# Differential attention run two heads at a time between the products that make q, k and v, with part of the output projection in its drain

## The reference

```python
q, k, v = jnp.split(h @ w_qkv, 3, axis=-1)       # h: 256 latent and 256 context tokens of 1024
s1 = einsum("bqhd,bkhd->bhqk", q1, k1) * scale    # 8 heads, each with two halves of 64
s2 = einsum("bqhd,bkhd->bhqk", q2, k2) * scale
p = softmax(s1) - lam * softmax(s2)
o = einsum("bhqk,bkhe->bqhe", p, v)
y = (rms_norm(o, subln_g) * (1 - lam_init)).reshape(b, s, D_MODEL) @ w_o
```

## Time and profile before

| what | value |
|---|---|
| median of 3 runs | 3429.49 us (3424.19 to 3432.53) |
| the profiled execution, its time | 3427.78 us |
| its span | 3426.5 us |
| mean granted clock of TensorE, of full speed | 0.962 |
| PE busy | 3164.6 us (92%) |
| DVE busy | 1747.6 us (51%) |
| ACT busy | 1449.8 us (42%) |
| POOL busy | 997.9 us (29%) |

### The profile page before, as it was taken

The page is one execution under the profiler, slowest core; times in us unless marked ns, Lnnn a source line. Parts: engine busy times, 40 slices in busy tenths (PEclk is TensorE's granted clock), DMA queues, the critical chain, the costliest instruction groups (busy, mean ns, idle before and its releaser), DMA issues.

```text
span 3426.5 us, 50565 instructions
## 1 busy us (share of the span) xinstructions
PE 3164.6 (92%) x21050; PEld 2685.3 (78%) x21050; DVE 1747.6 (51%) x2989; ACT 1449.8 (42%) x2388; POOL 997.9 (29%) x440
## 2 busy tenths in 40 slices
PE   5999998995789999799988989999999989999899
PEld 3777776773567777558988987777989977879899
DVE  3353334236453332665656655665456455654565
ACT  3442223224342222554445444655444456554443
POOL 0212212201111113003433432343443422434433
PEclk9999999996799999899999999999999999999999
DMA  8344444421145554104544543332445532334454
GB/s 282 123 135 160 160 160 144 163 74 50 37 148 172 172 169 149 53 25 136 185 133 130 190 138 111 99 99 87 151 145 176 181 117 85 101 99 151 147 183 148
DMA packets 469299, 459.97 MB, mean 134 GB/s; under 512 B 9040, under 2 KB 467664, under 8 KB 469072
## 3 DMA queue, kind: packets, MB, share of 16 engines
q1 hardware_dynamic: 465760, 453.32, 41.7%
q10 hardware_dynamic: 3312, 3.42, 0.3%
HBM read 455.66 MB, written 1.05 MB: 133 GB/s over the span
## 4 chain that ended last, share of the span: by engine, by line
PE 78%; DVE 11%; ACT 6%; issue 3%; POOL 1%; DMA 0%; ACTq 0%; DVEq 0%; POOLq 0%; SPq 0%
PE bank L398 22%; PE bank L399 21%; PE bank L400 21%; PE bank L442 3%; ACT wh L345 2%; DVE wl L361 2%; DVE hl L706 1%; PE bank L1403 1%; DVE sm L1249 1%; PE bank L1394 1%; PE bank L2141 1%; PE bank L1015 1%; PE bank L456 1%; DVE bc L2181 1%; POOL sq L514 1%
## 5 line engine op out<-in xcount | busy, mean ns | idle before, releaser
L373 POOL TENSOR_TENSOR wl<-raw,wh 128x768 fp32r<-128x768 f32 (+1 forms) x336 | 880.1, 2620 | 2148.2 <-ACT wh L345 2138.3
L345 ACT ACTIVATE wh<-raw 128x2048 fp32r<-128x2048 f32 x336 | 636.2, 1894 | 326.8 <-PE bank L400 311.4
L361 DVE TENSOR_TENSOR wl<-raw,wh 128x1280 fp32r<-128x1280 f32 (+1 forms) x336 | 499.0, 1485 | 425.2 <-ACT wh L345 416.3
L398 PE MATMUL bank<-nh,wh 128*128 128x272 f32 (+1 forms) x1712 | 509.9, 298 | 23.6 <-DVE nl L1726 22.8
L398 PE MATMUL bank<-xh,wh 128*128 128x512 f32 (+2 forms) x1312 | 463.8, 353 | 44.5 <-ACT xh L562 32.9
L400 PE MATMUL bank<-nh,wl 128*128 128x272 f32 (+1 forms) x1712 | 497.3, 290 | 0.0
L399 PE MATMUL bank<-nl,wh 128*128 128x272 f32 (+1 forms) x1712 | 495.8, 290 | 0.0
L399 PE MATMUL bank<-xl,wh 128*128 128x512 f32 (+2 forms) x1312 | 456.0, 348 | 0.0
L400 PE MATMUL bank<-xh,wl 128*128 128x512 f32 (+2 forms) x1312 | 455.0, 347 | 0.0
L398 PEld LDWEIGHTS bank<-nh,wh 128*128 128x128 f32 x1712 | 330.4, 193 | 40.1 <-issue 37.8
L398 PE MATMUL bank<-hh,wh 128*128 128x512 f32 (+1 forms) x1024 | 350.3, 342 | 3.4 <-DVE X L614 1.9
(11 more groups left out here) (408 smaller groups left out, 5634.1 us busy)
## 6 DMA issues: line engine op xcount, KB each, us to landing
raw<-in_mlp_w SPq DMA_DIRECT2D x128, 1024.0 KB, 5.3
raw<-in_mod_w SPq DMA_DIRECT2D x83, 1024.0 KB, 5.2
raw<-in_w_in SPq DMA_DIRECT2D x60, 1024.0 KB, 5.3
raw<-in_w_mlp_up SPq DMA_DIRECT2D x32, 1024.0 KB, 5.7
raw<-in_w_mlp_down SPq DMA_DIRECT2D x32, 1024.0 KB, 5.3
raw<-in_w_in SPq DMA_DIRECT2D x34, 512.0 KB, 4.1
raw<-in_w_ssd_down SPq DMA_DIRECT2D x16, 1024.0 KB, 5.2
early<-in_mod_w SPq DMA_DIRECT2D x13, 1024.0 KB, 11.9
```

What stands on the lines that cost most here:

```text
L345: nc.scalar.activation(self.wtile(self.wh, c1), self.rawtile(c1), AF.Copy).then_inc(*up("act_wh", ("wh", c1)))
L361: nc.vector.tensor_tensor(l, r, h.bitcast(F32), ALU.subtract).then_inc(*up("dve_wl", ("wl_dve", c1)))
L373: nc.gpsimd.tensor_tensor(l, r, h.bitcast(F32), ALU.subtract).then_inc(*up("pool_wl", ("wl_pool", c1)))
L398: nc.tensor.matmul(o, ah, bh, start=first, stop=False)
```

## The change: what it does

Two heads' q, k and v are made by one chunk each, and the chunks now come in the order q0, k0, v0, q1, k1, v1 and so on. As soon as two heads are there, their units of attention run between quarters of the next chunks (a quarter is half a group of q or k, 12 matmuls, or one tile of v, 24 narrow ones): `beat` gives two steps for three quarters. Steps 0 to 26 stand there; steps 27 to 36 are the drain. In steps 29 to 32 of the drain stand the first six of eight tiles of four groups of `wo` (`pe_wo`); their last two tiles and the other four groups follow after step 36. One step holds, on PE: the turn of unit s-2, the scores of unit s, the product with v of unit s-3 and, every fourth time, the turn of a head's output.

Within a step the work is different too. The scores have one pair of banks of PSUM, not two. DVE no longer scales both exponentials: it joins them in one instruction and leaves the division by the first sum to ACT, which applies it in four copies of 128 columns per head. All copies to `dpt` are ACT's. The root is taken on DVE for each head, from an integer guess and three refinements, eleven small instructions before the scaling; ACT loads no tables for it. The low part of the output is one DVE instruction on the bank. Four modulation chunks that stood after chunks of `wo` stand in the drain (steps 27, 28, 34, 35).

```diff
+            for j in range(4):
+                for i, p in enumerate("qkv"):
+                    w(("qkv", p, j), a["diff_w_qkv"][0], 0, 8, 1024 * i + 256 * j, 256)
+                    mods(2, 3 * j + i, 3 * j + i + 1)
+            mods(2, 12, 16)
...
+    def beat(self, w, j, half):
+        n = 12 * j + 4 * "qkv".index(w) + half - 8
+        return 2 * (n // 3) + n % 3 // 2 if n >= 0 and n % 3 != 1 else None
...
+                    for half in range(4):
+                        m = half // 2
+                        if half % 2 == 0:
+                            o = self.pe_bank((0, 1), "dqk", w, 2 * j + m)
+                        cs = slice(128 * m, 128 * m + 128)
+                        for k in range(4 * (half % 2), 4 * (half % 2) + 4):
+                            ins = self.mm3(o[:], hi[:, k, cs], lo[:, k, cs], XH[:, k, :], XL[:, k, :], k == 0, k == 7)
+                        if half % 2:
+                            ins.then_inc(*up("pe_acc", ("acc", "dqk", w, 2 * j + m), *([("used", c)] if m else [])))
+                        elif roping:
+                            self.pe_diff_rope(*roping)
+                            roping = None
+                        if half == 1:
+                            self.pe_turn()
+                        self.pe_diff_step(self.beat(w, j, half))
...
+        for s in range(self.LAST_BEAT + 1, 37):
+            self.pe_diff_step(s)
+            if s == 28:
+                self.pe_turn()
+            if s in (27, 28, 34, 35):
+                self.pe_mod(self.ix["mod", 2, 12 + (27, 28, 34, 35).index(s)], (7,) if s < 30 else (3,), (6,))
+            if 29 <= s < 33:
+                self.pe_wo(s - 29, 0, 6)
+            if s == 29:
+                self.pe_turn()
+        for g in range(8):
+            self.pe_wo(g, 6 if g < 4 else 0, 8)
+            self.pe_turn()
...
+    def pe_diff_step(self, s):
+        n = s - 2
+        if 0 <= n < 32:
+            b = self.pe_bank((4,), "dt", n)
+            PE.wait_ge(*at("dp", n))
...
+        if s < 32:
+            for i in range(2):
+                b = self.pe_bank((2 + i,), "ds", s, i)
...
+        n = s - 3
+        if 0 <= n < 32:
+            PE.wait_ge(*at("dpt", n))
...
+        h, b = divmod(s - 8, 4)
+        if b == 0 and 0 <= h < 8:
+            b = self.pe_bank((6,), "dx", h)
+            PE.wait_ge(*at("dn", h))
...
+    def dve_diff_step(self, s):
+        if s < 32:
+            for i in range(2):
+                DVE.wait_ge(*at("acc", "ds", s, i))
+                nc.vector.tensor_reduce(mx[:, i:i + 1], self.place["ds", s, i][:, 0:w], AX, ALU.max).then_inc(*DVE.step())
...
+        h, b = divmod(s - 7, 4)
+        if b == 0 and 0 <= h < 8:
+            self.dve_diff_root(h)
...
+        if s < 32:
+            DVE.wait_ge(*at("de", s))
+            nc.vector.reciprocal(t[:, 0:1], ac[:, 1:2]).then_inc(*DVE.step())
+            nc.vector.reciprocal(self.dinv(s), ac[:, 0:1]).then_inc(*DVE.step())
+            nc.vector.scalar_tensor_tensor(out=t[:, 1:2], in0=t[:, 0:1], scalar=ac[:, 0:1], in1=self.nlam, op0=ALU.mult, op1=ALU.mult).then_inc(*DVE.step())
+            nc.vector.scalar_tensor_tensor(out=e1[:, 0:w], in0=e2[:, 0:w], scalar=t[:, 1:2], in1=e1[:, 0:w], op0=ALU.mult, op1=ALU.add
+                                           ).then_inc(*up("dve_dp", ("dp", s)))
```

More of the change, by code:

```diff
@@ L299, in homes @@
                 continue
-            while late and d > 3 and (late[0] < self.dense[d - 3] or c == wo and late[0] < wo):
+            while late and d > 3 and (late[0] < self.dense[d - 3] or c == self.ix["wo", 2] and late[0] < self.ix["mod", 2, 14]):
                 self.order.append(late.pop(0))
@@ L1081, in pe_diff @@
[L1081 to L1117, removed]
@@ new lines, in pe_wo @@
+    def pe_wo(self, g, k0, k1):
+        nc, at, up, PE = self.nc, self.T.at, self.T.up, self.PE
+        c = self.ix["wo", g // 2]
+        hi, lo = self.pe_take(c)
+        if k0 == 0:
+            self.pe_bank(((0,), (1,), (7,), (2,), (4,), (5,), (3,), (0,))[g], "wo", g)
+        cs = slice(128 * (g % 2), 128 * (g % 2) + 128)
+        for k in range(k0, k1):
+            YH, YL = self.dout(k)
+            PE.wait_ge(*at("dxh", k))
+            PE.wait_ge(*at("dxl", k))
+            ins = self.mm3(self.place["wo", g][:], hi[:, k, cs], lo[:, k, cs], YH, YL, k == 0, k == 7)
+        if k1 == 8:
+            ins.then_inc(*up("pe_acc", ("acc", "wo", g), *([("used", c)] if g % 2 else [])))
@@ L1188, in act_diff @@
+        for s in range(self.LAST_BEAT + 1, 37):
+            self.act_diff_step(s)
+            if s in (28, 35):
+                self.act_mod(self.ix["mod", 2, 13 if s == 28 else 15])
+            if s == 33:
                 self.act_split(self.ix["wo", 0])
@@ new lines, in dve_diff @@
+        for j in range(4):
+            for w in "qkv":
+                c = self.ix["qkv", w, j]
+                self.dve_split(c)
+                if w == "q" and j == 0:
+                    self.dve_diff_rope("q", 0)
+                    roping = "q", 1
+                else:
+                    for half in range(4):
+                        if roping and (half == 0 if w == "v" else half % 2 == 0):
+                            self.dve_diff_rope(*roping)
+                            roping = None
+                        if half == 1:
+                            self.dve_add()
+                        self.dve_diff_step(self.beat(w, j, half))
+                        if w != "v" and half % 2:
+                            roping = w, 2 * j + half // 2
+                self.dve_mod(c + 1)
@@ L1304, in dve_diff @@
+        for s in range(self.LAST_BEAT + 1, 37):
+            self.dve_diff_step(s)
+            if s == 28:
+                self.dve_add()
+            if s in (28, 35):
+                self.dve_mod(self.ix["mod", 2, 13 if s == 28 else 15])
+            if s == 29:
+                self.dve_add()
+            if s == 33:
                 self.dve_split(self.ix["wo", 0])
```

400 lines of the change are left out of this document (190 added, 210 removed).

## The result

| kernel | median | lowest to highest |
|---|---|---|
| before | 3430.28 us | 3424.19 to 3432.53 |
| changed | 3354.50 us | 3354.20 to 3355.39 |

The ratio is 0.9782 (95% interval 0.9765 to 0.9799): 75.8 us less, where 64.7 were forecast.

What follows compares the result with a forecast made beforehand. The prediction took a chain of waits to bound the attention, PE the rest. Work of 82.4 and 50.5, waits of 10 and 12.5, 2.4 of low clock and 1.6 made 159.4 us instead of 224.1: 3365 us, range 3350 to 3393.

Steps and rivals of the forecast that it cites:

- What bounds the kernel: In the attention no engine is full; a chain of waits through DVE and ACT leaves PE busy 104.93 of 169.30 us.
- Attention at full clock: PE's work for all 8 heads without waits: 82.4 us, 64.6 in steps 0 to 26 and 17.8 in the drain.
- Waits within the steps: PE's waits in steps 0 to 26, among the chunks: 10 us, at most 35 if DVE has nothing to spare.
- The walk: Third pair of heads' three chunks: 3.9 us of waits, 0.4 score banks, 1.3 turn of output, 2.2 turn of modulation row.
- The drain: Behind the last modulation chunk: 12.5 us of waits (2.7, 3.1, 6.7), plus 2.4 for twelve matmuls at the lower clock.
- DVE's fifth: Steps 0 to 26: DVE's queue takes 23.9 us against PE's 30, so DVE has a fifth to spare.
- The row that I feared: A 0.42 us DVE instruction took 1.74 beside POOL's split; up to 1.7 us of DVE per chunk, covered, nothing added.
- What goes to nothing: ACT's eight table loads, its extra copies to `dpt` and DVE's saved scaling lie on engines not full: no effect on time.
- DVE did not set the pace: Rival: DVE's small waits and locks make PE wait in every step, 35 us instead of 10: 3390 us; chance 0.20.
- The clock stayed at 0.99: Rival: clock stays low among the products, up to 110 us more at a full stay, 3470 us; chance 0.04.
- the change hides little: Rival: every long unit's chain sticks out by 3 us, some 50 us back: 3415 us; chance 0.05.
- everything is covered: Rival: no waits in the steps and no low clock: 3352 us; chance 0.05 (everything covered and lower).

Runs made afterwards that it cites:

- noint: Changed kernel with all attention steps behind the twelve chunks, the rest of the change kept: 3427.07 us.
- noint2: As noint, with two pairs of score banks and two banks for the turned exponentials, as before the change: 3407.89 us.
- banks: Changed kernel with the turn of a modulation row in bank 7 (the last one in bank 1) instead of bank 6: 3347.18 us.
- dve1: Changed kernel with one extra DVE instruction on an unused tile in each of the 32 steps: 3356.65 us.
- dve3: Changed kernel with three extra DVE instructions on an unused tile in each of the 32 steps: 3368.39 us.
- tables: Changed kernel, root still on DVE, with an unused Ln and Exp and their table loads on ACT at each root: 3361.24 us.
- rootact: Changed kernel with each head's root by Ln and Exp on ACT and one refinement on DVE: 3374.00 us.
- mods: As banks, with the drain's modulation chunks after steps 28, 30 and 34 and the last between groups of the output projection: 3347.43 us.
- warm: As noint, with three extra unused matmuls on PE in each of steps 0 to 28: 3422.41 us.
- best: As mods, with six tiles of a fifth group of the output projection behind step 34: 3348.39 us.

## Why the prediction was right, point by point

**What bounds the kernel.** Right: the chain through DVE and ACT, with PE idle, was the price of the attention, and most of it went when the steps stood among products. noint separates it, but not to one number. With the single banks in both, placing is worth 3427.1 less 3354.5, 72.6 us. Against noint2, which has the second banks that an unplaced attention has room for, it is worth 53.4, and the rest of the change 22.4 of the 75.8. A placed attention with second banks was not run.

**Attention at full clock: the term that was mis-sized.** The sum had 64.6 us for steps 0 to 26. Measured: from the first product to the last modulation chunk beside the weights 222.97 us, against 158.1 before, so 64.9 with the waits; less 7.9 of waits that is 57.0 of work, 7.6 less than the sum had. I had added the lengths of rows, and the timeline's lengths overlap. The rows of one short step among the products, in the changed kernel:

```profile
631.37 0.60 PE L1169 MATMUL bank<-ident,de 128*128 128x128 f32 x4
631.90 0.70 PE L1178 MATMUL bank<-dk,dq 64*128 64x256 f32 x4
632.53 1.16 PE L1189 MATMUL bank<-dv,dpt 128*128 128x128 f32 x8
```

The turn has a length of 0.60, and the scores start 0.53 later; theirs is 0.70, and the next starts 0.63 later. The products with v have 1.16, and what follows starts 0.91 to 1.16 later. The turn of four tiles, moreover, had 0.67 in the row that I used, which stood behind a wait. From start to start, the 27 scores, 25 turns of exponentials, 24 products with v and 5 turns of outputs of these steps take 54.6 us, 10 less than the 64.6. The work of the chunks around them takes 2.4 more than the 158.1 of before. Together that is the 7.6.

**Waits within the steps.** 10 were forecast and 7.9 measured, half of them in the places named: 1.9 before one modulation row's turn (forecast 2.2 in each of three groups of chunks), and 2.1 before three turns of outputs for the rope in the shared bank (forecast 1.3 in each). The other 3.9 came before turns of exponentials, for ACT to empty their single bank. The walk had nothing there; it had 0.4 in each group before the scores, where PE never waited. So the total came close with a different make-up, in part by luck. With the 7.6 above and 2.1 here, 9.7 of the 11.6 us between forecast and measurement (64.7 against 76.3 from norm to norm) are found, and the drain has 1.8.

**The drain.** From the last modulation chunk beside the weights to DVE's row after the sum: 84.8 us measured, 86.6 by the sum. Single waits: 1.9 for the first weights (2.7), 3.2 for the low part (3.1), 5.4 and 0.6 at the last head (6.7). The low clock came, but elsewhere: in steps 28 and 29 behind the 3.2 us pause (2.8 us, by comparison with banks), and on the last modulation chunk (1.94) and the turn behind it, with only the first two matmuls of the projection, not twelve (some 1.8 us). That is 4.6 us where the sum had 2.4; the overlap of the rows' lengths, here as above, hides the difference.

**DVE's fifth.** Right, by dve1 and dve3: DVE had room, and not much of it. The row that I feared came up as well. DVE's timeline with a rope instruction of 0.42 behind a split, in the changed kernel:

```profile
645.49 1.49 DVE L362 TENSOR_TENSOR wl<-raw,wh 128x1280 fp32r<-128x1280 f32 x1 [3.02 <-ACT wh L346]
646.90 0.42 DVE L1022 TENSOR_TENSOR tmp<-bank,rt 128x256 f32<-128x256 f32 x1
647.23 1.71 DVE L1023 TENSOR_TENSOR dq<-dq,rt 128x256 f32<-128x256 f32 x1
649.05 0.43 DVE L1026 TENSOR_TENSOR dq<-dq,tmp 128x256 f32<-128x256 f32 x1
```

It took 1.71 us, as in the earlier trace rows. One joining took 2.07, every other 0.75 at most. This was covered, as the sum had it: PE has no wait for a joined exponential.

**What goes to nothing.** Wrong in one place. I put the loads of tables that the change removes at nothing, since ACT is not full. On ACT alone they would have cost 5 to 7 us among the products (tables), and with DVE waiting for their result 20 (rootact). The sum was not hurt, because it described the new form; but anyone who kept the old root among the products would have lost a quarter of the gain.

**The rivals.** DVE did not set the pace. The clock stayed at 0.99 among the products (in full that rival's terms come to 3475, not the 3470 given). That the change hides little was off by 60 us. That everything is covered was off by 2.5 us only, yet PE waited 7.9 us in the steps and 12 in the drain and the clock did fall there: its number is near because the work itself was put too high in the sum, which this rival shares.

**Open.** Nothing here tries a shorter chain for the last head, which sets the longest pause that is left, nor a second bank for the turned exponentials in the drain, for which PE waits 4.0 us in mods.

## What to carry to other kernels

A chain through three engines with idle between its links is worth placing among dense matmuls even if that costs its second buffers: here the second banks were worth 19 us without cover, and with it PE's waits for the single bank of exponentials came to 4.8 us. Each engine works through its queue in order, so a wait inside a queue can cost more than the work that it waits for: here the root on ACT cost 20 us when DVE waited for it, and 5 to 7 when nobody did. When counting an engine's work from a timeline, take starts, not lengths. And count for a pause also what runs behind it: after the pause of 3.2 us here, the next pieces took 2.8 us more than at full clock.

## What the runs showed of the hardware

In warm, 87 extra matmuls in 29 steps lifted the granted clock of the attention from the 0.70 of noint to 1.00 and cost nothing, but brought back 4.7 us only. In best, the first matmuls placed into a pause started 0.43 us apart instead of 0.23, and with the late split that ate half of the gain. The loads of ACT's tables took 1.28 us each, every time. A DVE instruction of 0.42 with two inputs in SBUF took 1.71 us while a split of POOL ran.
